# Token attention of a two-block transformer: new score banks, new order of groups, new place for the modulation products

## The reference, cut to what matters

```python
def mixer_a(...):          # 8 heads of 64, 2 key/value heads: softmax over 768 keys
def mixer_b(...):          # 4 heads of 64: a window of 8 rows x 16 columns with a learned bias, and the 256 context keys
def mixer_c(...):          # 4 heads of two 32-wide halves: w = softmax(s0) - lam * softmax(s1), then rms_norm(o, g_sub)
x = x + gt1_x * (concatenate([oa, ob, oc]) @ w_out[l])
x = x + gt2_x * conv_ffn(modulate(rms_norm(x, g_norm2[l]), sh2_x, sc2_x), ...)
```

## Time and profile before

| | us |
|---|---|
| median of three runs | 3680.66 |
| span of the profiled execution | 3674.5 |
| `x` attention, layer 0 (first score to first matmul of the projection) | 233.9 |
| `x` attention, layer 1 | 227.7 |
| `c` attention, layer 0 (521.9 to 586.1) | 64.2 |
| TensorE busy | 3542.3 |

### The profile page before, as it was taken

The page is one execution under the profiler, slowest core; times in us unless marked ns, Lnnn a source line. Parts: engine busy times, 40 slices in busy tenths (PEclk is TensorE's granted clock), DMA queues, the critical chain, the costliest instruction groups (busy, mean ns, idle before and its releaser), DMA issues.

```text
span 3674.5 us, 50083 instructions
## 1 busy us (share of the span) xinstructions
PE 3542.3 (96%) x19796; PEld 2813.1 (77%) x19796; DVE 1740.4 (47%) x2922; ACT 1525.6 (42%) x2558; POOL 1458.9 (40%) x986
## 2 busy tenths in 40 slices
PE   7999898999999999899999989999999989999998
PEld 5776566888899776578887768878887768888886
DVE  5766634433344766633542686161114676162114
ACT  4445544433355446534332355443223345443222
POOL 4520023544488520035444435344444434434442
PEclk8999998999999999999999999999999999999999
DMA  7613512333365421523333213223333212313331
GB/s 229 159 48 116 172 47 69 98 98 96 94 183 173 122 54 36 161 84 97 98 95 98 75 35 100 85 71 97 97 96 79 75 41 81 103 58 102 94 98 58
DMA packets 642466, 355.59 MB, mean 97 GB/s; under 512 B 70469, under 2 KB 614841, under 8 KB 642233
## 3 DMA queue, kind: packets, MB, share of 16 engines
q1 hardware_dynamic: 630379, 339.66, 32.0%
q10 hardware_dynamic: 11854, 12.72, 1.2%
HBM read 346.28 MB, written 6.05 MB: 96 GB/s over the span
## 4 chain that ended last, share of the span: by engine, by line
PE 89%; DVE 5%; ACT 3%; issue 2%; DMA 1%; POOL 1%; SPq 0%; ACTq 0%; DVEq 0%
PE psum L850 68%; PE psum L1055 5%; PE psum L1088 3%; PE psum L1106 2%; PE psum L874 1%; DVE neg_max L1920 1%; ACT work L1507 1%; PE psum L1135 1%; PE psum L954 1%; PE psum L878 1%; PE psum L1010 1%; PE psum L905 1%; PE psum L897 1%; DMA w_ada_first<-in_w_ada_dram 1%; PE psum L1113 1%
## 5 line engine op out<-in xcount | busy, mean ns | idle before, releaser
L833 POOL TENSOR_TENSOR w_lo<-w_raw,w_hi 128x256 fp32r<-128x256 f32 (+3 forms) x936 | 1397.0, 1512 | 2140.3 <-ACT w_hi L1358 2139.9
L850 PE MATMUL psum<-h_hi,w_hi 128*128 128x512 f32 (+1 forms) x2864 | 1078.7, 377 | 2.5 <-POOL w_lo L833 1.5
L850 PE MATMUL psum<-h_lo,w_hi 128*128 128x512 f32 (+1 forms) x2864 | 1054.5, 368 | 0.0
L850 PE MATMUL psum<-h_hi,w_lo 128*128 128x512 f32 (+1 forms) x2864 | 1054.1, 368 | 0.0
L1358 ACT ACTIVATE w_hi<-w_raw 128x1024 fp32r<-128x1024 f32 (+1 forms) x546 | 570.9, 1047 | 651.3 <-PE psum L850 618.2
L850 PEld LDWEIGHTS psum<-h_hi,w_hi 128*128 128x128 f32 x2864 | 541.5, 189 | 115.4 <-issue 20.2
L850 PEld LDWEIGHTS psum<-h_lo,w_hi 128*128 128x128 f32 x2864 | 541.5, 189 | 97.3 <-issue 9.9
L850 PEld LDWEIGHTS psum<-h_hi,w_lo 128*128 128x128 f32 x2864 | 541.3, 189 | 89.7
L850 PE MATMUL psum<-hid_hi,w_hi 128*128 128x512 f32 (+1 forms) x1040 | 393.0, 378 | 2.2 <-POOL w_lo L833 1.6
L850 PE MATMUL psum<-hid_lo,w_hi 128*128 128x512 f32 (+1 forms) x1040 | 391.9, 377 | 0.0
L850 PE MATMUL psum<-hid_hi,w_lo 128*128 128x512 f32 (+1 forms) x1040 | 391.9, 377 | 0.0
(11 more groups left out here) (225 smaller groups left out, 4055.8 us busy)
## 6 DMA issues: line engine op xcount, KB each, us to landing
w_raw<-in_w_up_dram SPq DMA_DIRECT2D x132, 512.0 KB, 3.8
w_raw<-in_w_ff_dram SPq DMA_DIRECT2D x128, 512.0 KB, 3.9
w_raw<-in_w_in_dram SPq DMA_DIRECT2D x92, 512.0 KB, 3.9
w_raw<-in_w_ada_dram SPq DMA_DIRECT2D x80, 512.0 KB, 4.2
w_raw<-in_w_down_dram SPq DMA_DIRECT2D x48, 512.0 KB, 3.6
w_raw<-in_w_mkv_dram SPq DMA_DIRECT2D x32, 512.0 KB, 3.8
w_raw<-in_w_down_dram SPq DMA_DIRECT2D x24, 384.0 KB, 3.1
w_ada_first<-in_w_ada_dram SPq DMA_DIRECT2D x4, 2048.0 KB, 17.9
```

The costliest lines, as they stand in the source:

```text
L833: m = nc.gpsimd.tensor_tensor(WL[:, c % NSPLIT, k:k + step, :], RAW[:, c % NRAW, k:k + step, :], WH[:, c % NSPLIT, k:k + step, :].bitcast( ...
L850: m = pe.matmul(out_ap, lhs(a, k), rhs(b, k), start=(k == 0 and n == 0), stop=(k == nk - 1 and n == 2))
```

## The change

The attention of `x` gets a plan and a loop of its own on each engine; that of `c` keeps the old loop. What is done:

- Each lane has three banks (0 to 2, 3 to 5), which hold two regions of 768 columns, used by turns. The 512-key piece of a step's scores is one whole bank, and is issued at the end of the step before; the 256-key piece lies in the bank that both regions share.
- The order is mixer a (steps 0 to 15), mixer c (16 to 31), mixer b (32 to 39).
- In a plain or bias step the first eight transposes are written over the step's own scores, and the last four to bank 7. A differential step has its own six transposes in bank 7, in fills of four and two, two steps later.
- The reciprocal sums are spread, copied and applied for each query tile (128 columns), right after its product with the values.
- The bias table is masked by GpSimd before the attention and no longer by VectorE in steps 4 to 7. The bias is added to the long piece as soon as it is made.
- The norm's square root for both differential groups is taken once, in step 37, between the exponentials.
- Chunks of `w_ada` are four k-tiles by 256 columns. `x` has two of them in each of steps 0 to 15, in both layers; `c` has one in each of steps 0 to 15. A row block of 256 columns is finished in every step of `x`, and in every second step of `c`.
- In the `c` attention the outputs of all groups share one bank, and the first two chunks of its `w_out` are split in steps 16 and 17.

```diff
-            add(("ada", l, b, j), "w_ada", l, 2 * j, 2, [(0, 4 * P, 4 * P * b)])
+            add(("ada", l, b, j), "w_ada", l, 4 * j, 4, [(0, 2 * P, 2 * P * b)])
...
-    if key[0] != "att" or key[1] != "x":
+    if key[0] != "att" or step < 0:
         return []
-    l = key[2]
-    parts = [(l, b, j) for b in range(ADA_FIRST, 12) for j in range(4)]
-    if l == 0:
-        parts += [(1, b, j) for b in range(ADA_FIRST) for j in range(4)]
-    pair = step - ADA_LAST + len(parts) // 2
-    return parts[2 * pair:2 * pair + 2] if pair >= 0 else []
+    if key[1] == "x":
+        parts = [(key[2], b, j) for b in range(2 * ADA_FIRST, 24) for j in range(2)]
+        return parts[2 * step:2 * step + 2]
+    return [(1, b, j) for b in range(2 * ADA_FIRST) for j in range(2)][step:step + 1]
...
+            for m in range(4):
+                plain(m, 4, values(0))
+                groups.append(dict(tile=m, diff=False, last=len(steps) - 1, turn=len(turns) - 1))
+            for j in range(2):
+                for t in range(4):
+                    i = len(steps)
+                    for e in range(2):
+                        steps.append(dict(diff=True, lanes=[lane(64 * e + 32 * m, 32, 9 + j, 11 + j, t) for m in range(2)],
+                                          bias=None, half=e))
+                    turn([(i, 0), (i + 1, 0)], values(384 + 128 * j), t)
+                groups.append(dict(tile=6 + j, diff=True, last=len(steps) - 1, turn=len(turns) - 1))
+            for j in range(2):
+                plain(5 + j, 7 + j, values(P + 128 * j), [window(2 * j + m) for m in range(2)])
...
+            turned_at, pv_at = {}, {}
+            for i, st in enumerate(steps):
+                turned_at.setdefault(i + (2 if st["diff"] else 1), []).append(i)
+            for q, u in enumerate(turns):
+                u["pv_at"] = u["after"] + (3 if steps[u["after"]]["diff"] else 2)
+                pv_at.setdefault(u["pv_at"], []).append(q)
+            ada_at, side = {}, {}
+            for i in range(n):
+                for block in ada_last(S, i):
+                    ada_at[i + 1] = block
+            for o in diffs:
+                side[groups[o]["last"] + 5] = ("sum", o)
+            std_at = groups[diffs[-1]]["last"] + 6
+            for m, o in enumerate(diffs):
+                for half in range(2):
+                    side[std_at + 1 + 2 * m + half] = ("spread", (o, half))
+                groups[o]["hi_at"] = std_at + 3 + 2 * m
+            for o, g in enumerate(groups):
+                if not g["diff"]:
+                    g["hi_at"] = g["last"] + 3
...
+        def region(i, m):
+            lane = PS[:, 3 * m:3 * m + 3, :].rearrange("p b c -> p (b c)")
+            return lane[:, i % 2 * NK:i % 2 * NK + NK]
...
+        def keys_long(i):
+            return slice(0, SEQ) if i % 2 == 0 else slice(CTX, NK)
+        def keys_short(i):
+            return slice(SEQ, NK) if i % 2 == 0 else slice(0, CTX)
...
+        X_OUT, X_RECIP, X_SIDE = (PS[:, 6, a:b] for a, b in ((0, P), (P, 2 * P), (2 * P, 4 * P)))
...
-            att = dict(one_out=S[:2] == ("att", "x"), ada_bank={}, S=S, steps=steps, turns=turns, groups=groups, PT=PTt, nt=nt)
-            att["wide"] = any(st["nk"] > 512 for st in steps)
-            att["prob"] = PROBS[768 if att["wide"] else 512]
+            att = dict(one_out=S[0] == "att", ada_bank={}, S=S, steps=steps, turns=turns, groups=groups, PT=PTt, nt=nt)
...
+                    if c == IDS["qkv", "x", l][-1] + 1:
+                        pool.wait_ge(*at("tab_in", ("win", l)))
+                        for h in range(B_HEADS):
+                            nc.gpsimd.tensor_tensor(TB[:, h], TB[:, h], WINDOW.unsqueeze(1).broadcast_to([P, 14, 64]),
+                                                    ALU.add).then_inc(*mark("win_bias", (l, h)))
...
+            def ada_product(rows, w, nk, j):
 
                 for k in range(nk):
-                    g = 32 * (k + done) % P
-                    m = pe.matmul(PS[g:g + 2, bank, :], SILU[:, j + k, :], w(k), start=j + k < 4, stop=j + k >= last - 4)
...
+                def score_long(i):
...
+                    elif steps[i - 2]["diff"]:
+                        pe.wait_ge(*at("exp_done", (S, i - 2, 1)))
+                    else:
+                        pe.wait_ge(*at("pt_copied_act", (S, i - 2)))
+                        pe.wait_ge(*at("pt_copied_dve", (S, i - 2)))
+                    for m, (q, k) in enumerate(steps[i]["lanes"]):
+                        ins = pe.matmul(region(i, m)[:, keys_long(i)], q, k[:, 0:SEQ], start=True, stop=True)
+                    ins.then_inc(*mark("long_done", (S, i)))
+                def score_short(i, lanes):
+                    if i:
+                        pe.wait_ge(*at("exp_done", (S, i - 1, lanes[-1])))
+                    for m in lanes:
+                        q, k = steps[i]["lanes"][m]
+                        pe.matmul(region(i, m)[:, keys_short(i)], q, k[:, SEQ:NK], start=True, stop=True).then_inc(
+                            *mark("scores_done", (S, i, m)))
+                def turn_ada(i):
+                    block = att["ada_at"][i]
+                    pe.wait_ge(*at("ada_rows", block))
+                    pe.wait_ge(*at("exp_done", (S, i - 1, 0)))
+                    ada_turn(AROW, 2, lambda n: spare(i)[:, 2 * n:2 * n + 2]).then_inc(*mark("ada_turned", block))
+                def turn_plain(i):
+                    for m in range(2):
+                        pe.wait_ge(*at("exp_done", (S, i, m)))
+                        for n in range(4):
+                            ins = pe.transpose(region(i, m)[:, keys_long(i)][:, n * P:(n + 1) * P],
+                                               probs(i, m)[:, n * P:(n + 1) * P], IDENT)
+                        ins.then_inc(*mark("group_turned", (S, i, m)))
...
+                def turn_mixed(i, fill):
+                    if fill:
+                        pe.wait_ge(*at("pt_copied_act", (S, i, 0)))
+                    else:
+                        pe.wait_ge(*at("mix_step", (S, i, "mixed")))
...
+                score_long(0)
+                for i in range(att["length"]):
+                    turned = att["turned_at"].get(i, ())
+                    plain = [j for j in turned if not steps[j]["diff"]]
+                    mixed = [j for j in turned if steps[j]["diff"]]
+                    if i in att["ada_at"]:
+                        turn_ada(i)
+                    if i < len(steps):
+                        score_short(i, (0,) if mixed else (0, 1))
+                    for j in mixed:
+                        turn_mixed(j, 0)
+                    if mixed and i < len(steps):
+                        score_short(i, (1,))
+                    for j in mixed:
+                        turn_mixed(j, 1)
+                    for j in plain:
+                        turn_plain(j)
+                    out_free(i)
+                    if i in att["side"]:
+                        side(i)
+                    for q in att["pv_at"].get(i, ()):
+                        value(q)
+                    ada(S, i, ada_rows, X_SIDE)
+                    if i + 1 < len(steps):
+                        score_long(i + 1)
...
+                def exp(i, m):
+                    act.wait_ge(*at("neg_max", (S, i, m)))
+                    if i >= 2 and not steps[i - 2]["diff"]:
+                        act.wait_ge(*at("group_turned", (S, i - 2, m)))
+                    elif i >= 2 and m == 0:
+                        act.wait_ge(*at("mix_step", (S, i - 2, "mixed")))
+                    elif i >= 2:
+                        act.wait_ge(*at("group_turned", (S, i - 2, 1)))
+                    c = (2 * i + m) % 4
+                    nc.scalar.activation(probs(i, m), region(i, m), ACT.Exp, bias=NMAX[:, c:c + 1],
+                                         accum_out=SUMS[:, i % NSUM, m:m + 1]).then_inc(*mark("exp_done", (S, i, m)))
...
+                def recips(i):
+                    for block in ada_last(S, i):
...
+                            act.wait_ge(*at("ada_turned", ada_rows[-1]))
...
+                    for q in att["pv_at"].get(i, ()):
+                        act.wait_ge(*at("pv_done", (S, q)))
+                        if q >= 2:
+                            act.wait_ge(*at("o_step", (S, q - 2)))
+                        nc.scalar.activation(recip_rows(q), X_RECIP, ACT.Copy).then_inc(*mark("recip_copied", (S, q)))
...
+                    if i == att["std_at"]:
+                        act.wait_ge(*at("side_taken", (S, i - 1)))
+                        nc.scalar.activation(SUBS[:, :, :], SUBS[:, :, :], ACT.Sqrt, bias=EPSC[:, 0:1],
+                                             scale=1.0 / HEAD).then_inc(*mark("sub_std", S))
+                n = len(steps)
+                for i in range(att["length"]):
+                    if 0 < i <= n and not steps[i - 1]["diff"]:
+                        copy_plain(i - 1)
+                    if i < n:
```

(49 more changed lines are left out.)

325 lines of the change are left out of this document (256 added, 69 removed).

## The result

| | before | after |
|---|---|---|
| median of the runs, us | 3681.01 (4 runs, 3677.1 to 3684.03) | 3753.65 (4 runs, 3747.23 to 3757.71) |
| span of the profiled execution | 3674.5 | 3755.8 |
| `x` attention, layer 0 | 233.9 | 262.2 |
| `x` attention, layer 1 | 227.7 | 267.3 |
| `c` attention | 64.1 | 77.0 |

The ratio is 1.0199, 95% interval 1.0184 to 1.0215: slower by 72.6 us. The forecast was 3703 us, slower by 23; its range ended at 3728. The sign was right, the size was a third of it.

What follows compares the result with a forecast made beforehand. TensorE was taken to bound plain steps, not differential ones; `x` layers +4.2 and +10.4, `c` +9: +23.6 on 3674.5, 3698, with 6.2 around it 3704, stated as 3703 us. Range 3671 to 3728 (its own 3688 to 3718).

Steps and rivals of the forecast that it cites:

- Plain steps, 6.33 us: Plain steps of `x` with two chunks, 16 per layer: TensorE's pieces sum to 6.33 us each.
- Differential steps, 5.15 us: Differential steps of `x` without products, 16 per layer: 5.15 us each, bounds 3.7 and 6.0.
- the walk: Differential steps: scaling waits for ACT's reciprocals' copy, queued behind a copy of four transposed tiles; two steps take 10.3 us.
- Rival "half clock": TensorE's gaps in differential steps let the clock fall, doubling its work in half the cycles: up to +31 us; chance 0.17.
- three signs under "I am wrong if": Differential steps at 4 us, 256-column products far under 0.97 per pair, or the `c` attention not growing.
- Handover, 2 us: In each `x` layer, the passage from differential to bias steps: 2 us.
- Bias steps: Last steps of `x`, without products, 8 per layer: 5.6 us each, bounds 4.6 and 6.0.
- Tail: End of each `x` attention: transposes, copies, values, reciprocals, scaling and handover, 5.0 us.
- Steps 16 and 17: First two steps after the plain ones in `x`, with plain turns still to do: 4.7 and 3.7 us.
- `c`, +9 us: The `c` attention grows by 9 us from chunks, row blocks and splits, four products hidden; bounds +4 and +14.
- Root: Step 37's square root on ACT's chain, with a table load before and one back: 2.9 us.
- Rival "freed": The scaling's wait doesn't bind; differential steps run at DVE's load, 3.9 us, saving 35: 3669 us; chance 0.20.

Runs made afterwards that it cites:

- held at full clock: Kernel after with two thrown-away 512-column TensorE products ahead of the long piece in every second differential step: 3718.76 us.
- the two edits before it: Kernel after with the reciprocals' copy first on ScalarE and two thrown-away 512-column products in every second differential step: 3704.22 us.
- wait, clock and handover mended: Kernel after with reciprocals' copy first, last differential value one pass earlier, one thrown-away 256-column product in every second differential step: 3679.71 us.

## Why the prediction was wrong, step by step

- *Plain steps, 6.33 us.* Right: 6.34 us in both layers. The products of such a step on TensorE, kernel after, from their start to that of the long piece, take 0.98 us where the forecast had 0.97:

```profile
300.00 1.05 PE L1053 MATMUL psum<-w_raw,silu_c 128*2 128x256 f32 x16
300.98 1.13 PE L1269 MATMUL psum<-qk_t 64*128 64x512 f32 x4
```

- *Differential steps, 5.15 us.* This step failed, and by its clock: the walk took every piece of TensorE's work at full speed. The wait is as walked, and held at full clock the 14 steps took 71.1 and 72.7 us against the forecast's 74.2. In the kernel after they took 86.8 and 90.5, 28.9 us over it, at 0.72 and 0.63.
- *Rival "half clock".* It had this mechanism, priced it at up to 31 us and got 0.17. So close a size is partly luck: it had half of the cycles slowed, where a mean of 0.72 and 0.63 means half speed in 56% and 74% of the time. Its condition was wrong: TensorE never idled for some microseconds in these steps, the longest gap was 0.77 us. (It was VectorE that stood still for 4.87.) "`x` held 0.97 with similar steps" was the wrong witness: before, those steps carried the modulation products, and without them the late steps of the kernel before fell from 0.96 and 0.92 to 0.72 and 0.70. There is a slip in its sum as well: 3703 and 31 make 3734, not 3731, and either lies beyond the stated range, which ends at 3728. None of the three signs under "I am wrong if" looked at the clock.
- *Handover, 2 us.* Failed. From the exponential of step 32 to that of step 39 it took 54.7 and 56.2 us against about 47.1 (7 x 5.6, 2 and 5.9): +16.6 us. Bias steps by themselves were right (5.7 for 5.6), and so was the reason given for them. What was missed is that last differential and first bias value meet in one pass; moving one gave 9.7 us. Part of the rest went with the two edits before it, which took layer 0 from 54.7 to 50.8.
- *Tail.* The forecast had 5.0 us behind the last exponentials, about 7.5 when counted from the start of the first of them. It took 10.1 in both layers, +5.2. *Steps 16 and 17* together took 9.4 for 8.4, +1.0 in each layer.
- *`c`, +9 us.* 12.8. Inside its bounds of 4 and 14; four products were called hidden in differential steps, and the chunks cost 0.8 each on average. The part that it gave to a change of tile shape is shown by no run.
- *Root.* 2.9 us, right.
- *Outside the attention.* The two projections of `x` took 1.6 and 1.8 us less. All that lies behind the second attention, its projection included, took 2.7 us more in this execution.
- The four largest misses, 28.9, 16.6, 5.2 and 3.8, make 54.5 of the 57.7 us by which the span of 3755.8 is over the sum's 3698.1.
- *Rival "freed".* Wrong for the kernel as written, as the wait bound. But with wait, clock and handover mended the steps take 3.8 and 4.9 us by turns, 4.3 on average, with 0.53 us of thrown-away work in each pair. So its 3.9 is nearer than 5.15 to what the order is worth once nothing stands in it.

## What to carry to other kernels

When a walk of waits leaves TensorE gaps in every round, even gaps of under a microsecond, the clock belongs into the same sum, not into a rival: price the work of that round at both clocks. Small work that fills such gaps can be worth its own time, as in the late steps of the kernel before, so look at the granted clock of the steps it leaves before moving it away. It doesn't always come back with the work: modulation products put into the new differential steps did not hold the clock reliably, the thrown-away ones did. And where each engine waits in its program's order, list for each copy which pass of the other engine makes its input; one that stands behind a copy of the next pass delays all that follows.
